# Seven half-size products for the band projections of a streaming encoder step

## What is computed

```
q_b, k_b, v_b, z_b = h @ w_in columns, 1024 each      # h: RMSNorm(x), 1056 x 1024
q_b = rms_norm(q_b per head of 64, b_q_g);  k_b likewise with b_k_g
prompt: chunk c of 64 frames reads itself and the 8 chunks before it
sample: the 32 frames read 512 cached rows and themselves
s = q k^T / 8 + bias[head, clip(distance, -128, 128)];  p = softmax(s)
o_b = (p v) * silu(z_b);    k_b, v_b of the last 512 frames and of the sample are outputs
```

## Time and profile before

| | us |
|---|---|
| median of three runs | 3466.81 (3466.38 to 3468.75) |
| the profiled execution | 3467.14 |
| its span | 3465.2 |

### The profile page before, as it was taken

How to read it: one execution, slowest core, us unless ns; L and a number is a source line. 1 busy time by engine, 2 the same in 40 slices (tenths; PEclk the granted TensorE clock), 3 DMA queues, 4 the chain that set the end, 5 groups by cost and what they waited for, 6 DMA issues and landing times. The chain is left out here.

```text
span 3465.2 us, 47876 instructions
## 1 busy us (share of the span) xinstructions
PE 3396.3 (98%) x16717; PEld 2579.3 (74%) x16717; DVE 1292.4 (37%) x3168; ACT 1123.3 (32%) x2870; POOL 503.4 (15%) x506
## 2 busy tenths in 40 slices
PE   8999999999899999999999999899999999999999
PEld 5777777777577877777776667688888888766676
DVE  3555555555323333333321224334433433310233
ACT  4343433333234343433310143123323333210242
POOL 1454345445000000000001001100000000010000
PEclk9999999999999999999999999999999999999999
DMA  5211021112311113112252101111111011470101
GB/s 161 53 40 39 26 29 34 32 31 95 106 39 46 41 37 39 36 43 96 71 192 69 61 1 38 52 49 54 43 52 53 24 53 53 137 232 31 37 1 51
DMA packets 245820, 206.03 MB, mean 59 GB/s; under 512 B 20127, under 2 KB 222783, under 8 KB 245655
## 3 DMA queue, kind: packets, MB, share of 16 engines
q1 hardware_dynamic: 240302, 194.29, 20.3%
q10 hardware_dynamic: 5360, 9.67, 0.7%
HBM read 157.95 MB, written 45.99 MB: 59 GB/s over the span
## 5 line engine op out<-in xcount | busy, mean ns | idle before, releaser
L510 PE MATMUL gdn_pj<-hT,Wb 128*128 128x352 f32 x1536 | 516.7, 462 | 5.5 <-ACT gdn_zraw L747 3.9
L1462 PE MATMUL band_pj<-hT,Wb 128*128 128x384 f32 (+1 forms) x1152 | 384.4, 462 | 4.9 <-ACT band_rs L1603 3.0
L510 PEld LDWEIGHTS gdn_pj<-hT,Wb 128*128 128x128 f32 x1536 | 266.3, 192 | 95.1 <-ACT gdn_zraw L747 4.5
L1462 PEld LDWEIGHTS band_pj<-hT,Wb 128*128 128x128 f32 x1152 | 206.1, 191 | 86.3 <-ACT band_rs L1603 7.1
L1872 PE MATMUL gla_pj<-gla_TX,gla_S 128*128 128x256 f32 (+1 forms) x736 | 191.2, 393 | 0.0
L1872 PE MATMUL gla_pj<-hT,gla_S 128*128 128x256 f32 (+1 forms) x736 | 187.3, 393 | 0.0
L1872 PEld LDWEIGHTS gla_pj<-hT,gla_S 128*128 128x128 f32 x736 | 139.3, 190 | 26.2
L1648 ACT ACTIVATE band_E<-band_NS,band_nm 128x576 f32<-128x576 f32 (+9 forms) x136 | 89.8, 661 | 211.1 <-DVE band_nm L1726 211.0
L1872 PEld LDWEIGHTS gla_pj<-gla_TX,gla_S 128*128 128x128 f32 x736 | 138.2, 190 | 26.2
L1216 POOL TENSOR_TENSOR x_kept<-gdn_AT,gdn_level 128x384 f32<-128x384 f32 x144 | 144.2, 1032 | 35.6 <-DVE gdn_TT L998 18.5
L1492 PE MATMUL band_pj<-Wb,hT 128*128 128x128 f32 x1152 | 144.2, 275 | 0.0
(11 more groups left out here) (469 smaller groups left out, 6167.2 us busy)
## 6 DMA issues: line engine op xcount, KB each, us to landing
Wb<-in_l_w_in_dram SPq DMA_DIRECT2D x95, 512.0 KB, 6.6
fin_xT<-x_features SPq DMA_DIRECT2D x16, 528.0 KB, 7.2
fin_R<-o_features SPq DMA_DIRECT2D x16, 528.0 KB, 9.4
Wb<-in_l_w_mkv_dram SPq DMA_DIRECT2D x8, 1024.0 KB, 5.4
Wb<-in_l_w_out_dram SPq DMA_DIRECT2D x16, 512.0 KB, 4.1
o_features<-gla_OF ACTq DMA_DIRECT2D x14, 528.0 KB, 7.6
gla_Wv<-in_l_w_in_dram SPq DMA_DIRECT2D x7, 1024.0 KB, 5.3
gdn_GB<-gate_rows SPq DMA_DIRECT2D x8, 544.0 KB, 3.7
```

Of the source, the lines that this page charges most:

```text
L510: mm = pe.matmul(pj[:, m % 2, 0:w], W[:, j, k, :], hT[:, k, c0:c0 + w], start=k == 0, stop=k == KD - 1)
L1462: mm = pe.matmul(out[:, 0:w], W[:, BAND_SLOT[j], k, :], hT[:, k, c0:c0 + w], start=k == 0, stop=k == KD - 1)
```

## The change

The q and k projections of a pair are computed together by seven products of half size in place of eight, and so are z and v; v therefore comes out feature-major (`vraw`) and is turned by nine TensorE transposes in three jobs (`vt`). Per pair the stream is 28 products of four k, one `ck`, five norm jobs (four of 512 columns that take 256 of each token half, one of 64 for the sample columns), two `ko` and three `vt`: 123 steps. P3, P7 and P2 are added by VectorE, the others copied by ScalarE, so the signal `proj_out` becomes `act_out` and `dve_out`. VectorE also makes the four weight sums of each product group, after its adds of P7 and P2, and once, at the stage's start, the token sums. Squares come from the copied sums. The token sums `TX` take the place of `early` in memory: five of the early features' blocks are loaded early, the rest when the last products are done, and x goes into `raw`.

```
-        STREAM = ([("q", 0), ("q", 1), ("q", 2), ("k", 0), ("nq", 0), ("nq", 1), ("nq", 2), ("k", 1), ("k", 2), ("z", 0),
-                   ("nk", 0), ("nk", 1), ("nk", 2), ("z", 1), ("z", 2), ("ko", 0), ("ko", 1), ("ck", 0)]
-                  + [("v", t) for t in range(TILES)])
+        STREAM = (products(0, 0) + [("ck", 0)] + products(0, 1) + [("n", 0), ("n", 1)] + products(1, 0) + [("n", 2), ("n", 3), ("n", 4)]
+                  + products(1, 1) + [("ko", 0), ("ko", 1), ("vt", 0), ("vt", 1), ("vt", 2)])
+        T_FIRST, T_OPS = {"P5": 2, "P6": 3, "P7": 1, "P4": 4}, 9
...
 # TensorE
-                        wait(pe, proj_out, n * J + m - 1)
+                        evicted(pe, n, m - 2)
+                        if kind in FAST:
+                            x, u = i
+                            A1, A2 = pair_weights(x)
+                            if u == 0:
+                                if kind == "P1":
+                                    pair_loaded(pe, n, x)
+                                elif kind in FAST_SUMS:
+                                    pe.wait_ge(w_made, n * 8 + x * 4 + FAST_SUMS.index(kind) + 1)
+                            if isinstance(n, int) and n == 0 and x == 0:
+                                if u == 0 and kind in T_FIRST:
+                                    pe.wait_ge(t_made, T_FIRST[kind])
+                                elif u == 1 and kind == "P1":
+                                    pe.wait_ge(t_made, T_OPS)
...
+                            if i == 0:
+                                last_of(1, 1, n, pe)
+                                pe.wait_ge(padded, 1)
+                            for b, t in enumerate(range(4 * i, min(4 * i + 4, TILES))):
+                                mm = pe.transpose(out[:, 128 * b:128 * b + 128], vraw[:, 128 * t:128 * t + 128], ident[:, :])
...
 # ScalarE
+                        if (kind, i) == ("P6", (0, 1)):
+                            square(n, 0)
+                            square(n, 1)
+                        elif (kind, i) == ("P6", (1, 0)):
+                            for s in (2, 3, 4):
+                                square(n, s)
...
 # VectorE
+                def add(n, p, m, again):
+                    kind, (x, u) = STREAM[m]
+                    dve.wait_ge(proj_done, n * J + m + 1)
+                    evicted(dve, n, place[{"P3": "P6", "P7": "P5", "P2": "P1"}[kind], (x, u)])
+                    dst = fast_place(target(p, x), UNITS_OF[u], kind)
+                    dve.tensor_tensor(dst, dst, pj[:, (p * J + m) % 2, 0:fast_width(UNITS_OF[u], kind)], ALU.add).then_inc(dve_out, 1)
+                    if u and (again or x == 0):
+                        following = (n, 1) if x == 0 else (n + 1, 0)
+                        for i in {"P3": (), "P7": (0, 1), "P2": (2, 3)}[kind]:
+                            combine(*following, i)
...
+                DVE_JOBS = sorted([(ends[m], m) for m in BY_DVE] + [(ends[place["n", 1 if s < 2 else 4]] + 1 + s % 2, J + s) for s in range(NORMS)])
...
 # SP, follow
+                    sp.wait_ge(proj_done, n * J + place["P4", (1, 1)] + 1)
+                    for j in (2, 3):
+                        if more:
+                            load_w(n + 1, j)
+                        elif more is False:
+                            early_w(sp, W, early_ld, w_out, j, BAND_SLOT[j])
+                    if more is False:
+                        early_rows = o_dram.rearrange("(k p) t -> p k t", p=128)
+                        sp.dma_start(o_rest, early_rows[:, FIRST_K:H_A - 1, 0:384]).then_inc(eo_ld[0][1], 16)
+                        for c in (1, 2):
+                            c0, w = EARLY_PARTS[c]
+                            sp.dma_start(o_parts[c - 1], early_rows[:, 0:H_A - 1, c0:c0 + w]).then_inc(eo_ld[c][0], 16)
+                        sp.wait_ge(normed, PAIRS * NORMS)
+                        for i in range(2):
+                            early_x(sp, x_dram, x_stage, x_ld, i)
```

More of the change, by code:

```diff
@@ new lines, in band, with evicted @@
+        BY_DVE = [m for m, (kind, _) in enumerate(STREAM) if kind in FAST_DVE]
+        BY_ACT = [m for m in range(J) if m not in BY_DVE]
+        JD, JA = len(BY_DVE), len(BY_ACT)
+        NORMS = 5
+        T_FIRST, T_OPS = {"P5": 2, "P6": 3, "P7": 1, "P4": 4}, 9
+        def evicted(eng, n, m):
+            if m < 0:
+                m += J
+                n = n - 1
+                if isinstance(n, int) and n < 0:
+                    return
+            if m in BY_DVE:
+                eng.wait_ge(dve_out, n * JD + BY_DVE.index(m) + 1)
+            else:
+                eng.wait_ge(act_out, n * JA + BY_ACT.index(m) + 1)
@@ L1430, in _ @@
                 pair(5, 1, True, True)
[L1431 to L1434, removed]
+                early_o(sp, o_dram, o_first, eo_ld[0][0], 0, 0, FIRST_K)
                 pair(6, 0, False, False)
-                early_w(sp, W, early_ld, w_out, 3, BAND_SLOT[3])
                 sp.wait_ge(st_o, (PAIRS - 1) * 16)
@@ L1673, in _ @@
                 act.preload_act_table_set("natural_log_exp_and_others")
-                for m in range(J):
-                    if m == place["nq", 0]:
+                for m in BY_ACT:
+                    if m == place["n", 0]:
                         act.wait_ge(consts, 2)
@@ L1709, in pair, with combine @@
-                def pair(n, p, more):
-                    left = list(range(6)) if more else []
-                    def norms(steps):
-                        while left and ends[place["nq" if left[0] < 3 else "nk", left[0] % 3]] <= steps:
-                            normalise(n + 1, 1 - p, left.pop(0))
+                def combine(n, x, i):
+                    A1, A2 = pair_weights(x)
+                    if i == 0:
+                        pair_loaded(dve, n, x)
+                    if x:
+                        dve.wait_ge(proj_done, n * J + place[FAST_SUMS[i], (0, 1)] + 1)
+                    else:
+                        wait(dve, proj_done, (n - 1) * J + place[FAST_SUMS[i], (1, 1)] + 1)
+                    fast_weights(dve, A1, A2, S4, i, w_made, n * 2 + x)
@@ new lines, in _, with job, pair, jobs @@
+                DVE_JOBS = sorted([(ends[m], m) for m in BY_DVE] + [(ends[place["n", 1 if s < 2 else 4]] + 1 + s % 2, J + s) for s in range(NORMS)])
+                def job(n, p, m, again):
+                    if m < J:
+                        add(n, p, m, again)
+                    else:
+                        normalise(n, p, m - J)
+                def pair(n, p, more, again=True):
+                    left = list(DVE_JOBS) if more else []
+                    def jobs(steps):
+                        while left and left[0][0] <= steps:
+                            job(n + 1, 1 - p, left.pop(0)[1], again)
@@ L1855, in fast_width, with fast_product, fast_place @@
     return unit[1] if name in ("P1", "P2", "P4") else unit[2]
+def fast_product(pe, bank, left, right, unit, name, done):
+    w = fast_width(unit, name)
+    for k in range(FAST_K):
+        mm = pe.matmul(bank[:, 0:w], left(name, k), right(name, k, unit[0], w),
+                       start=name in ("P1", "P5", "P2") and k == 0, stop=k == FAST_K - 1, skip_group_check=True)
+        if k == FAST_K - 1:
+            mm.then_inc(done, 1)
+        yield
+def fast_place(out, unit, name):
+    f, c = {"P1": (0, 0), "P5": (1, SPLIT), "P6": (0, SPLIT), "P4": (1, 0), "P3": (0, SPLIT), "P7": (1, SPLIT), "P2": (0, 0)}[name]
+    c += unit[0]
+    return out(f)[:, c:c + fast_width(unit, name)]
 def fast_steps(pe, pj, left, right, unit, g, copied, added, done, operands):
     for name in FAST:
-        w, bank = fast_width(unit, name), fast_bank(unit, name)
         operands(name)
```

297 lines of the change are left out of this document (176 added, 121 removed).

## The result

| | before | after |
|---|---|---|
| median of the runs, us | 3467.11 (3466.38 to 3468.75) | 3445.70 (3444.3 to 3446.86) |
| ratio, 95% interval | | 0.9937 (0.992 to 0.9955) |
| span of the profiled execution | 3465.2 | 3444.9 |
| band stage begins | 926.15 | 921.88 |
| first stream | 67.65 | 64.67 |

The change gains 21 us; 30 were forecast. By stage: first stream -3.0, seven pairs -13.3, last pair +0.4, all that stands ahead of the band -4.3 (no edited line; see the experiment on the kernel before).

What follows compares the result with a forecast made beforehand. TensorE's matmul columns were taken to bound the pairs (busy 98.5 of 99.9 us). -60 + 9.2 + 9.0 + 0.7 + 3.9 + 1 + 6.4 = -30 us against 3467.14 gave 3437; forecast span 3428 to 3446, range 3419 to 3454.

Steps and rivals of the forecast that it cites:

- the clock: TensorE's clock falls to half behind waits before the first transposes, 1.7 us each; half of eight taken, +6.4 us.
- the start: Start of the band stage: VectorE makes the token sums first, so P2 waits for its add 3.9 us, once.
- the clock falls at every boundary: Rival: the clock halves at all eight pair boundaries, costing 13.6 us, whole 3444 us; chance 0.12.
- The pair as a whole: Each band pair, all terms together: about 96 us in place of 99.9.
- the column term: TensorE products in each pair: 58.6 us removed, 50.1 and 1.0 added; gain 7.5 us a pair, 60 for eight.
- The pair's end: Last product, k- and v-transposes behind the last attention unit wait on ScalarE copies: 1.15 us, eight times, +9.2.
- The first transpose: Next pair's first transpose waits for softmax behind ScalarE's gate: 1.3 us more, to some 2.0, seven times, +9.0.
- Evictions: Rival: products wait for late ScalarE or VectorE copies and adds; 3457 us at 0.1 us each, 3496 at 0.3; chance 0.14.
- the norm bursts: Two bursts of norm work in a pair delay copies and a gate by 0.8 us; +0.1 a pair net.
- The last pair: Early feature loads, now issued later, and x behind them delay the last pair: +1 us, range 0 to 5.

Runs made afterwards that it cites:

- the experiment on the kernel before: The kernel before the change, run once more unedited: 3466.68 us.
- a_loads_behind: Changed kernel with the loads of the pair after next's z and v weights issued behind the OF store and the values' loads, not ahead of the stores: 3424.06 us.
- g_shifted: `a_loads_behind` with every load of the z and v weights starting 128 columns earlier: 3424.93 us.
- b_two_of: Changed kernel with two OF buffers in place of one, and three blocks of early features loaded early in place of five: 3440.43 us.
- i_one_ahead: `a_loads_behind` with the load of z's weights put back ahead of the stores of KO, VT and OF: 3430.75 us.

## Why the prediction was right, and where it wasn't

The time fell into the range, 8.7 us above the forecast and 0.3 inside its own span of 3428 to 3446. That nearness is partly luck: one missing term of +20.2 stands against two that were too high (the clock by 5.3 outside that term, the start by 1.6) and a gain of 4.3 from elsewhere. The rival *the clock falls at every boundary* had 3444, which is nearer, but its condition failed: behind waits of the size that it priced (1.76 us measured) the clock never fell.

*The pair as a whole, right; two of its terms were off and cancel.* 99.9 - 7.5 + 1.15 + 1.3 + 0.1 = 94.9 by the terms without the clock; the four undisturbed pairs took 94.9 to 95.2. By the distance of starts, idle time taken out, the q, k, z and v products of pair 1 took 59.1 us before and the seven-product ones 51.2 after, with 1.3 for turning v: a gain of 6.7 against 7.5 (58.6, 50.1 and 1.0 in the sum), and busy time fell by 6.2. So the column term was 0.8 to 1.3 us too high; part of it may be that each new wait shows the full length of the record before it (0.38) in place of its distance (0.216). The waits, 1.4 us before, are 2.9 after, where +2.55 was forecast: 1.1 too high. On the Trainium skill's figures (TensorE: Matmul & The Clock Gate, Back-to-back issue gap) the products would have gained 5.4 us before the transposes: the traces have 59.1 - 51.2 = 7.9.

*The pair's end, right.* 1.0 us of waits in the v transposes (0.4 + 0.6 in the rows above) against 1.15.

*The first transpose, right.* 1.76 us against 2.0; moving the gate showed the chain to be the cause.

*Evictions, right to be a rival only.* In an undisturbed pair no product waits for ScalarE or VectorE (pair 1's waits above), and the 0.8 us put on the norm bursts didn't come.

*The start, over-sized.* 3.9 us were forecast, 2.26 measured, since the token sums ended 1 us sooner and the products 0.5 later. But the clock fell behind it: these rows are the wait and the four microseconds behind it, and then the same in `a_loads_behind`, where the wait was 1.70:

```profile
935.07 2.63 PE L2025 MATMUL band_pj<-hT,Wb 128*128 128x256 f32 x8 [2.26 <-DVE band_raw L1805]
936.00:940.00 4.00, 4.00 (x12) 3.21 (x12) 0.42 (x1) 0.00 (x0) 0.00 (x0) 0.57 0.44 138
...
936.00:940.00 4.00, 3.96 (x21) 3.29 (x20) 0.42 (x1) 0.98 (x2) 0.46 (x1) 1.00 0.63 192
```

The first stream took 64.67 and 62.99 us: 0.56 of that is idle, 1.1 is clock. The fall alone, 3.4 us at half, costs 1.7; against it, the stage's start ran 5.4 us at half clock in `a_loads_behind` and 4.2 in after.

*The clock, wrong in place.* +6.4 stood for half of eight boundaries. At 1.76 us idle none fell, in 4 pairs of after and 7 of `a_loads_behind`, so this term was nothing. The falls that were there, behind idles of 3.32, 7.27 and 6.14 us in the long pairs and 2.26 at the start, followed from the stalls and the start. Those in the long pairs cost 7.0 us of TensorE's busy time (95.2 + 94.6 + 94.1 - 3 x 92.3), about as much as the term had, by another cause.

*The last pair, right in sign.* +0.4 against +1.

*The step that failed is a term left out.* The prediction followed SP's queue at the start and in the last pair, where loads visibly moved, and gave the seven pairs none. It should have read `follow` for them: `load_w` for j = 2 and 3 at one wait, the stores of KO, VT and OF behind it. Before, each slot had its own moment. Pairs 3, 4 and 5 cost 99.7 + 104.6 + 101.3 - 3 x 95.15 = 20.2 us, 13.2 of it idle and 7.0 clock. Without it the sum of the other terms as measured (-3.0, 7 x -4.75, +0.4, -4.3) is -40.2; with 1.7 less in the first stream, as in `a_loads_behind`, -41.9, and that kernel's median is 43 below before.

## What to carry to other kernels

When a change lets several buffers come free at one moment, write down which transfers are now issued there and what is queued behind them; loads that nobody needs soon go behind stores that free a buffer. Where equal stretches of a loop differ in length, compare their waits, granted clock and transfers before anything else. And trace each microsecond of a gain to its stage: here a fifth of it came from one that nobody had edited.

## What the runs showed of the hardware

- Two slices of 128 columns of a weight matrix took 15.5 to 16.2 us to land (median of two loads of 0.5 MB), where the other loads of this kind took 8 to 12, and the slowness moved with the address (`g_shifted`). The DMA engines were busy for 0.98 of the 15 us behind the issue, against 0.48 for the next two slices.
- With the DMA engines wholly busy (share 1.01 from 1371 to 1386 in after), SP took 2.5 to 4.8 us to issue a store that otherwise takes 0.4. ScalarE stood up to 4.75 us (`b_two_of`) behind a jump in its code, and a packet of the instruction queue started 1.7 to 1.8 us ahead of the end of each such gap.
- In the band, TensorE's clock fell to half (1.2 GHz) behind an idle of 2.23 us (`i_one_ahead`, pair 3) and of 2.26 to 2.63 at the first stream's P2 in four traces, behind one of seven of 2.28, and behind none of 1.48 to 1.77. The length of the idle doesn't settle it: at 27 us of the span, with other short idles ahead, the clock fell behind 1.6 us in eleven of thirteen traces, and at an idle of 2.09 us in the next stage (2030 in before, 2010 in after) in eight of thirteen. The Trainium skill (TensorE: Matmul & The Clock Gate, Why this matters for your kernels) advises against gaps above some 3 us; the falls here after 2.23 and 2.26 us show that a shorter one can be enough.
